# Value products in two passes of two query blocks, with a new order of copy, low part, exponent and scaling

## The reference

```python
q = einsum("btd,de->bte", rmsnorm(x), w_q)            # 16 heads of 64
s = einsum("bqhd,bkhd->bhqk", q_blk, k) * 64 ** -0.5  # blocks of 128 queries
s = s + fq_blk[..., :, None] - fk_t[:, :, None, :]    # forget bias
pr = softmax(where(kpos <= pos_blk, s, -inf))
o = einsum("bhqk,bkhd->bqhd", pr, v)
x = x + einsum("bte,ed->btd", o, w_o)
```

## Time and profile before

| | |
|---|---|
| median of 3 runs | 2847.16 us (2846.88 to 2847.24) |
| profiled execution | 2846.86 us, span 2845.0 us |
| PE busy | 2764.6 us (97%) |
| DVE busy | 1366.8 us (48%) |
| ACT busy | 836.1 us (29%) |
| attention pairs | from 1226 us to 1886 us of the span |

### The profile page before, as it was taken

One profiled execution on the slowest core, in us unless ns is written; L12 is line 12 of the kernel. 1 busy time (PEld: TensorE's weight loads), 2 busy tenths in 40 slices (PEclk: granted clock), 3 DMA queues, 4 the chain that ended last, 5 costly groups with the idle time before them and its releaser, 6 DMA issues.

```text
span 2845.0 us, 43288 instructions
## 1 busy us (share of the span) xinstructions
PE 2764.6 (97%) x18039; PEld 2693.4 (95%) x18039; DVE 1366.8 (48%) x1841; ACT 836.1 (29%) x1334; POOL 119.1 (4%) x82
## 2 busy tenths in 40 slices
PE   8999999999999999999999999879999999999998
PEld 8999999999999999989888889779999999999998
DVE  6876444344244244455556655554542442442444
ACT  6765221121111112334444444442211110111121
POOL 1000100000000000310000000002000000000000
PEclk9999999999999999999999999899999999999999
DMA  3113111111111111233322323111111111111112
GB/s 134 40 44 99 48 45 42 50 50 37 57 45 40 51 45 40 57 103 83 90 75 63 94 87 98 53 41 50 42 42 54 45 39 54 45 39 53 45 44 78
DMA packets 91342, 166.49 MB, mean 59 GB/s; under 512 B 18066, under 2 KB 55154, under 8 KB 91026
## 3 DMA queue, kind: packets, MB, share of 16 engines
q1 hardware_dynamic: 91154, 163.72, 19.1%
HBM read 141.60 MB, written 13.70 MB: 55 GB/s over the span
## 4 chain that ended last, share of the span: by engine, by line
PE 88%; DVE 4%; issue 4%; ACT 2%; DMA 1%; DVEq 0%; SPq 0%; ACTq 0%
PE psum L339 78%; PE psum L1160 2%; PE psum L1108 2%; PE psum L1132 2%; DVE SB L1565 1%; DMA NF<-nf_scratch 1%; PE psum L1090 1%; DVE PTL L1592 1%; PE psum L1147 1%; ACT PTH L888 0%; DVE X L1648 0%; ACT SB L872 0%; PE psum L958 0%; PE psum L1074 0%; PE psum L960 0%
## 5 line engine op out<-in xcount | busy, mean ns | idle before, releaser
L339 PE MATMUL psum<-XH,WH 128*128 128x352 f32 x2904 | 641.1, 329 | 1.8 <-issue 1.8
L339 PE MATMUL psum<-XH,WL 128*128 128x352 f32 x2904 | 628.2, 324 | 0.0
L339 PE MATMUL psum<-XL,WH 128*128 128x352 f32 x2904 | 627.6, 324 | 0.0
L321 ACT ACTIVATE WH<-WR 128x1024 fp32r<-128x1024 f32 (+2 forms) x217 | 215.4, 993 | 1037.0 <-PE psum L339 1025.1
L339 PEld LDWEIGHTS psum<-XH,WL 128*128 128x128 f32 x2904 | 498.3, 188 | 1.6
L339 PEld LDWEIGHTS psum<-XL,WH 128*128 128x128 f32 x2904 | 493.8, 188 | 1.6
L339 PEld LDWEIGHTS psum<-XH,WH 128*128 128x128 f32 x2904 | 488.7, 189 | 5.0 <-issue 2.3
L1448 DVE TENSOR_TENSOR X<-psum,X 128x1056 f32<-128x1056 f32 x63 | 79.2, 1257 | 371.2 <-PE psum L339 371.2
L330 DVE TENSOR_TENSOR WL<-WR,WH 128x1024 fp32r<-128x1024 f32 (+2 forms) x217 | 246.0, 1134 | 11.7 <-ACT WH L321 11.3
L339 PE MATMUL psum<-FYH,WH 128*128 128x352 f32 x1134 | 245.3, 324 | 0.0
L339 PE MATMUL psum<-FYH,WL 128*128 128x352 f32 x1134 | 244.5, 323 | 0.0
(11 more groups left out here) (228 smaller groups left out, 3266.3 us busy)
## 6 DMA issues: line engine op xcount, KB each, us to landing
WR<-in_wfi SPq DMA_DIRECT2D x96, 512.0 KB, 3.5
WR<-in_wfo SPq DMA_DIRECT2D x64, 384.0 KB, 3.0
WR<-in_wa SPq DMA_DIRECT2D x24, 512.0 KB, 3.6
WR<-in_wqkv SPq DMA_DIRECT2D x24, 512.0 KB, 4.8
X<-in_xT SPq DMA_DIRECT2D x16, 528.0 KB, 5.3
CC<-in_ck SPq DMA_DIRECT2D x128, 64.0 KB, 1.9
NF<-nf_scratch SPq DMA_DIRECT2D x16, 512.0 KB, 4.6
CC<-in_cv SPq DMA_DIRECT2D x128, 64.0 KB, 1.9
```

The costliest lines, as they stand in the source:

```text
L321: nc.scalar.activation(WH[:, par, 0:n], WR[:, par, 0:n], ACT.Copy).then_inc(w_hi, 1)
L339: mm = nc.tensor.matmul(psum[0:m, 3 * slot + c, 0:CH], w, x[:, k, c * CH:(c + 1) * CH], start=(k == 0 and part == 0), stop=(k == nk - 1 an ...
```

## The change

The value products are made for two query blocks at a time (a double, units 2d+1 and 2d+2, in the new order 7 6, 1 0, 5 4, 3 2). The values lie as low and high part side by side, 128 stationary columns, and each key block gets two matmuls of 256 moving columns: one with `PTH` and one with `PTL`. The results high and low stand in different halves of the PSUM partitions; ACT moves one half out (`o_half`), DVE adds the other (`add_halves`, `o_read`). The product of a double stands ahead of `turn` in its even slot, the decode product ahead of `turn(1)` in slot 2. In the pairs 0 to 6 ACT copies the high part of unit v-1 ahead of the exponent of v, and DVE takes its low part ahead of the scaling of v, from slot 2 on. The K tile is read in slot 12 behind the scaling. `KSTEPS` is spread anew. The PSUM homes are exchanged: `S_ps` 0 and 1, `O_ps` 2, projections 3 to 5, `T_ps` 6 and 7.

The last pair has code of its own: two `T_ps` (`T_alt` in the banks of the projections), its own second bias tile, logits one slot ahead, scaling and low part one slot later, the old order on ACT, and the splits of the first output tiles and the first output projection step inside it.

```diff
-BLOCKS = [7, 0, 6, 1, 5, 2, 4, 3]
+BLOCKS = [7, 6, 1, 0, 5, 4, 3, 2]
-KSTEPS = [2, 1, 2] + [1] * 14 + [3, 2]
+KSTEPS = [2, 1, 1, 1, 2, 1] + [1] * 6 + [2, 1, 1, 1, 1, 2, 2]
+PVS = 1 + NQB
@@ SyncE, pair
-                sp.wait_ge(s_read, u0 + 1 + NQB)
-                sp.dma_start(NF[:, :], ins["nf"][2 * hp + 1, :].partition_broadcast(P)).then_inc(nf_ld, 16)
+                if last:
+                    sp.wait_ge(k_out, 16 * NHP)
+                else:
+                    sp.wait_ge(s_read, u0 + 1 + NQB)
+                sp.dma_start((NF_last if last else NF)[:, :],
+                             ins["nf"][2 * hp + 1, :].partition_broadcast(P)).then_inc(nf_ld, 16)
@@ ScalarE, pair
+                    if v < 2 or c == NHP - 1:
+                        if v < UNITS:
+                            exponent(v)
+                        if v == 0:
+                            values_hi(c, t)
+                        copy_probs(v)
+                    else:
+                        copy_probs(v)
+                        if v < UNITS:
+                            exponent(v)
...
+                    elif v >= 5 and v % 2:
+                        d = (v - 5) // 2
+                        h = UNIT_OF[2 * d + 2][0]
+                        act.wait_ge(pv_done, PVS * c + d + 2 + 2 * PVS * t)
+                        nc.scalar.activation(out_double(d, hp), o_double(d)[HALF[1 - h], :],
+                                             ACT.Copy).then_inc(o_half, 1)
@@ ScalarE, last pair
+                    if c == NHP - 1 and v == UNITS - 1:
+                        act.wait_ge(qk_done, UNITS * NHP)
+                        act.wait_ge(k_out, 16 * NHP)
+                        o_split_hi(0)
+                    if c == NHP - 1 and v == UNITS:
+                        o_split_hi(1)
@@ TensorE, pair
+                def product(d):
+                    v = 2 * d + 2
                     h, i = UNIT_OF[v]
                     pe.wait_ge(pt_lo, (UNITS - 1) * c + v + 2 * (UNITS - 1) * t)
-                    pe.wait_ge(o_read, u0 + v)
-                    cols = slice(HD * h, HD * (h + 1))
-                    for kb in range(i + 1):
-                        keys = slice(P * kb, P * (kb + 1))
-                        for x, y, part in ((VH, PTH, 0), (VH, PTL, 1), (VL, PTH, 2)):
-                            mm = nc.tensor.matmul(O_ps[0:HD, 0:P], x[:, kb, cols], y[v % 2][:, keys],
-                                                  start=(kb == 0 and part == 0), stop=(kb == i and part == 2))
+                    if d == 0:
+                        pe.wait_ge(o_half, PVS * c + 1 + 2 * PVS * t)
+                    wait(pe, o_read, NQB * c + d + 2 * NQB * t if c or d else 0)
+                    for kb in range(i + 2):
+                        b = 0 if kb <= i else 1
+                        vv = VV[:, kb, 2 * h:2 * h + 2, :].rearrange("p a d -> p (a d)")
+                        for y, part in ((pt_buf(PTH, c, d), 0), (pt_buf(PTL, c, d), 1)):
+                            mm = nc.tensor.matmul(o_double(d)[:, P * b:2 * P], vv,
+                                                  y[:, kb, b:2, :].rearrange("p a q -> p (a q)"),
+                                                  start=(kb == 0 and part == 0), stop=(kb == i + 1 and part == 1),
+                                                  skip_group_check=True)
                     mm.then_inc(pv_done, 1)
+                if last:
+                    logits(0)
+                    values()
+                    logits(1)
+                    for v in range(1, UNITS + 2):
+                        if v + 1 < UNITS:
+                            logits(v + 1)
+                        if v == 2:
+                            decode_product()
+                        if v <= UNITS:
+                            turn(v - 1)
+                        if v == UNITS + 1:
+                            pe.wait_ge(w_ready, J_O + 1)
+                            pe.wait_ge(acc_read, J_O)
+                            pe.wait_ge(pt_lo, (UNITS - 1) * NHP - 1)
+                            o_k_step(0)
+                        if v >= 4 and v % 2 == 0:
+                            product((v - 4) // 2)
+                    return
                 for v in range(UNITS + 2):
                     if v < UNITS:
                         logits(v)
...
                     for _ in range(KSTEPS[v]):
                         project()
+                    if v == 2:
+                        decode_product()
+                    elif v >= 4 and v % 2 == 0:
+                        product((v - 4) // 2)
                     if 1 <= v <= UNITS:
                         turn(v - 1)
-                    if v >= 2:
-                        product(v - 2)
@@ VectorE, pairs 0 to 6
+                for v in range(UNITS + 1):
+                    if v < UNITS:
+                        maximum(v)
+                    if v - 1 in SPLIT_SLOTS:
+                        lo_weights(dve, J_QKV + 3 * c + 4 + SPLIT_SLOTS.index(v - 1), 6, t)
+                    if v == 5:
+                        dve.wait_ge(job_done, J_QKV + 3 * c + 4 + 6 * t)
+                        scaled(dve, 1, QS[:, :]).then_inc(acc_read, 1)
+                    if v >= 2:
+                        probs_lo(v - 1)
+                    if v < UNITS:
+                        normalise(v)
+                    if v == 12:
+                        dve.wait_ge(job_done, J_QKV + 3 * c + 5 + 6 * t)
+                        dve.wait_ge(k_out, 16 * (c + 1) + 32 * t)
+                        scaled(dve, 1, KS[:, :]).then_inc(acc_read, 1)
+                    if v == 0:
+                        values_lo(c, t)
+                    if v >= 5 and v % 2:
+                        add_halves(c, t, (v - 5) // 2)
+                    spread(v)
```

More of the change, by code:

```diff
@@ L859, in pair, with exponent, copy_probs @@
                     keys_hi(0, 0, 0)
-                for v in range(UNITS + 2):
+                def exponent(v):
+                    rows, n = (2 * NS, DK) if v == 0 else (P, P * (UNIT_OF[v][1] + 1))
+                    act.wait_ge(s_read, u0 + v + 1)
+                    nc.scalar.activation(SB[0:rows, v % 2, 0:n], SB[0:rows, v % 2, 0:n], ACT.Exp,
+                                         bias=nmax[0:rows, v:v + 1], scale=-1.0,
+                                         accum_out=lsum[0:rows, v:v + 1]).then_inc(e_done, 1)
+                def copy_probs(v):
+                    if v == 1:
+                        act.wait_ge(t_done, u0 + v)
+                        T0 = t_unit(c, 0)
+                        nc.scalar.activation(PTD[:, 0:4 * NS], T0[:, 0:4 * NS], ACT.Copy)
+                        nc.scalar.activation(PTD[0:NS, 4 * NS:6 * NS], T0[0:NS, 4 * NS:6 * NS],
+                                             ACT.Copy).then_inc(pt_hi, 1)
+                    elif 2 <= v <= UNITS:
+                        act.wait_ge(t_done, u0 + v)
+                        if v >= 4 and v % 2 == 0:
+                            act.wait_ge(pv_done, PVS * c + v // 2 - (c == NHP - 1) + 2 * PVS * t)
+                        nc.scalar.activation(pt_unit(PTH, c, v - 1), t_blocks(c, v - 1), ACT.Copy).then_inc(pt_hi, 1)
+                for v in range(UNITS + 3):
                     if v == 2:
@@ L868, in pair @@
                         keys_hi(c + 1, t, 0)
-                    if v < UNITS:
-                        rows, n = (2 * NS, DK) if v == 0 else (P, P * (UNIT_OF[v][1] + 1))
-                        act.wait_ge(s_read, u0 + v + 1)
-                        nc.scalar.activation(SB[0:rows, v % 2, 0:n], SB[0:rows, v % 2, 0:n], ACT.Exp,
-                                             bias=nmax[0:rows, v:v + 1], scale=-1.0,
-                                             accum_out=lsum[0:rows, v:v + 1]).then_inc(e_done, 1)
@@ new lines, in pair, with o_split_hi @@
+                    if c == NHP - 1 and v == UNITS:
+                        o_split_hi(1)
+            def o_split_hi(d):
+                nc.scalar.activation(YO[:, d, 0, :], X[:, d, :], ACT.Copy).then_inc(o_hi, 1)
+            over_pairs(act, pair)
+            o_split_hi(2)
+            act.wait_ge(pv_done, PVS * NHP)
+            act.wait_ge(v_out, 16 * NHP)
+            for d in range(3, KT - 1):
+                o_split_hi(d)
+            act.wait_ge(o_half, PVS * NHP)
+            act.wait_ge(o_read, NQB * NHP)
@@ new lines, in pair, with maximum @@
+                    add_halves(c - 1, t, NQB - 1)
+                def maximum(v):
+                    rows, n = (2 * NS, DK) if v == 0 else (P, P * (UNIT_OF[v][1] + 1))
+                    bias = DM if v == 0 else NF_last if c == NHP - 1 and v > NQB else NF
+                    wait(dve, t_done, u0 + max(v - 1, 0))
+                    if v in (1, 1 + NQB):
+                        dve.wait_ge(nf_ld, 16 * (2 * c + 1 + (v > 1)) + 64 * t)
+                    wait_apart(dve, qk_done, u0 + v + 1, logits_seen)
+                    nc.vector.tensor_tensor_reduce(
```

(9 more changed lines are left out.)

240 lines of the change are left out of this document (121 added, 119 removed).

## The result

The changed kernel takes **2861.5 us** (median of 5, 2857.2 to 2864.1) against 2847.2 before: +14.3 us, ratio 1.0043, interval 1.0028 to 1.0058. Run once more beside the experiments it took 2864.4 us, ratio 1.0064, interval 1.0047 to 1.0081. It is slower, as forecast, but by just under half of the 28.8 us forecast. The profiled execution took 2861.53 us with a span of 2859.7.

A forecast was written before the change was run, and what follows sets the result against it. The prediction took middle pairs as bound by PE (97% busy overall) and the last pair by the engine-to-engine chain. Span 2845.0 + 44 (seven pairs) - 15 (last pair) = 2874, forecast 2876 us, range 2851 to 2895.

The forecast's parts named there:

- Products: Value products on PE in a middle pair: 14.3 us before, 10.4 after, so 3.9 us less PE work.
- Waits: PE's waits in a middle pair: 14.2 us after the change against 3.7 before, 10.5 us more.
- turn 2: Transposes between blocks 7 and 6, first head: PE waits 1.7 us for the scaling behind copy and low part.
- logits 10: Second head's logits: the bias is loaded after the maximum of unit 8, so PE waits 1.8 us.
- additions, 8/10/14/16: Products in slots 8, 10, 14, 16 wait for the previous double's addition on DVE: 0.8, 0.4, 0.6, 1.3 us.
- K tile: V projection's first step, slot 13: PE waits 2.1 us because the K tile is read behind a late scaling.
- the layouts' difference: Middle pair laid out by hand at full clock, old against new order: +6.3 us a pair, +44 us over seven.
- The last pair: Last pair up to the first output projection step: 15 us gained, with 8 and 24 as ends.
- The chain is covered: Rival: in middle pairs only PE work counts, saving 3.9 us each, giving 2805 us; chance 0.09.
- Only the old length of chain counts: Rival: scaling as if ready before the low part, 2.7 us more per middle pair, giving 2851 us; chance 0.13.
- The waits bring the low clock: Rival: a further low-clock stretch after the decode product costs up to 3 us a pair, giving 2897 us; chance 0.12.
- Passes paced by weight loads: Rival: two-pass product matmuls take 0.19 us each, +4.8 us per pair on the forecast, giving 2910 us; chance 0.04.

The follow-up runs named there:

- e4: Changed kernel with output halves, their additions and the K tile's scaling moved ahead within their slots in pairs 0 to 6: 2833.0 us, ratio 0.9957.
- e5: e4 (new order kept) with the projection's steps spread anew over the slots: 2813.5 us, ratio 0.9879.
- e7: Kernel before with only the new order on ScalarE and VectorE, from slot 2 on in pairs 0 to 6: 2843.1 us, ratio 0.9990.
- e6: e4 with the old order and the projection's steps spread anew for that order: 2812.5 us, ratio 0.9880.
- e15: e6 with the projection's steps spread as in the changed kernel: 2819.2 us, ratio 0.9904.
- e1: Changed kernel with the old order on both ScalarE and VectorE in pairs 0 to 6: 2830.3 us, ratio 0.9949.
- e10: Changed kernel without the products with the probabilities' low parts in pairs 0 to 6, so its output differs: 2844.6 us, ratio 0.9984.
- e9: Changed kernel with only the output halves and their additions moved ahead within their slots in pairs 0 to 6: 2858.3 us, ratio 1.0038.
- e13: Changed kernel with only the K tile's scaling moved ahead of the low part in slot 12, pairs 0 to 6: 2849.1 us, ratio 1.0015.
- e2: Changed kernel with the old order on ScalarE alone in pairs 0 to 6: 2874.8 us, ratio 1.0100.
- e3: Changed kernel with the old order on VectorE alone in pairs 0 to 6: 2920.6 us, ratio 1.0264.
- e8: Changed kernel with its last pair run like the others: old order, one home for turned units, late output splits: 2891.1 us, ratio 1.0156.

## Why the prediction had the direction right and the size wrong

**Products: more saved than forecast.** I took 0.125 us for 256 columns; they take 0.120. I took 0.112 us for the 16 of 128 columns, from a decode product whose matmuls have 8 columns; they take 0.061 and 0.113 by turns. For this and the following terms I took, for each matmul of a pair, the middle value over seven pairs of the time to the next matmul's start. The products sum up to 15.0 us before (forecast 14.3) and 9.5 after (10.4): 5.5 us less and not 3.9. About 0.4 of the 15.0 is low clock: the first product of 24 matmuls, right behind the decode product, takes 1.9 us and, outside low clock, 1.4. The Trainium skill's rule (TensorE: Matmul & The Clock Gate, Back-to-back issue gap), by which it would have been 9.9, does not fit: the 98 ns estimated from that page stand against 120 measured.

**Waits: right in place, too large in size.** In the same sheet PE's waits over 0.2 us are, us a pair:

```
                      forecast  measured
turn 2                   1.7       0.6
turn 10                  1.7       1.7
turns 6, 14              1.6       1.7
logits 4                 0.9       0.8
logits 10                1.8       1.3
additions, 8/10/14/16    3.1       2.3   (0.9, 0, 0.4, 1.0)
K tile                   2.1       2.0
all waits, before        3.7       2.1
all waits, after        14.2      11.6
```

Each wait that was named is there, and turn 10, turns 6 and 14, logits 4 and the K tile came out within 0.1 us. The error is in turn 2, in logits 10 and in the additions, of which slot 10's doesn't show. The growth is 9.5 us a pair, not 10.5.

**Transposes and logits**, entered at no change, grew by 1.5 us a pair in amounts under 0.2 us each. Most of it is not gaps but clock: 0.9 us of it lies in slot 2, where the transposes of unit 1 now follow the decode product and run at low clock in four of the seven pairs. Typical pair: -5.5 + 9.5 + 1.5, about +5.4 (81.9 to 87.3).

**Low clock costs in full where PE sets the pace, and nothing where PE waits for the chain.** The layout has the full clock and left everything else as it was. To see what the clock does, take one slot in pairs that differ in it; columns as in the earlier trace rows. Slot 2 (logits 2, one step, decode product, turn 1) of pairs 2 and 3 in the changed kernel, where PE doesn't wait:

```profile
1410.64:1420.05 9.41, 9.41 (x58) 8.87 (x57) 3.06 (x5) 3.21 (x6) 1.90 (x1) 0.77 0.36 105
1503.75:1511.11 7.36, 7.36 (x58) 6.83 (x57) 3.06 (x5) 3.21 (x6) 0.14 (x1) 1.00 0.46 130
```

Slot 3 (logits 3, one step, turn 2) of pairs 0 and 4 there, then of pair 1 in e4, which has the same work in that slot:

```profile
1243.64:1248.94 5.30, 3.71 (x22) 3.11 (x20) 3.63 (x6) 3.84 (x5) 0.97 (x1) 0.86 0.44 123
1598.97:1604.28 5.31, 5.04 (x22) 4.29 (x20) 3.63 (x6) 3.42 (x5) 0.00 (x0) 0.57 0.44 126
1328.42:1333.62 5.20, 3.00 (x22) 2.47 (x20) 3.63 (x6) 3.85 (x5) 0.92 (x1) 1.00 0.40 114
```

PE is busy for 3.0 to 5.0 us in it, by the clock, and the slot takes 5.2 to 5.3 us all the same: the scaling sets its end. In e4's pair 1, at the full clock, turn 2 starts 1.7 us late, as laid out; in the changed kernel 1.1 of the 1.7 us are filled by PE's own slower work. In e5, where three steps stand in slot 3 and PE doesn't wait, it is 6.5 us at 0.83 and 7.5 at 0.71:

```profile
1570.19:1576.66 6.47, 6.47 (x40) 6.35 (x38) 3.64 (x6) 3.22 (x4) 1.35 (x1) 0.83 0.45 129
1649.87:1657.36 7.49, 7.49 (x40) 7.37 (x38) 3.63 (x6) 3.21 (x4) 1.90 (x1) 0.71 0.40 112
```

**The step that failed: the layouts' difference, +6.3 us a pair, entered as the growth of a pair.** The prediction read what the trace had above the layout (2.3 us in its pair, 2.4 on average) as the low clock behind the decode product, and left it as it was. But pair 4 of the kernel before had no low clock at all and took 82.3 us, not 81.0, longer than pair 5, which had it:

```profile
1563.78:1646.10 82.32, 79.19 (x636) 72.00 (x635) 48.36 (x100) 35.93 (x79) 5.69 (x3) 1.00 0.29 85
1646.10:1728.03 81.93, 80.01 (x636) 73.50 (x634) 48.12 (x100) 35.87 (x79) 5.69 (x3) 0.98 0.29 85
```

"Undisturbed" in the next table is a pair put together slot by slot, each slot at the middle length that it has in pairs where no low clock falls into it (where there is none such, in all pairs; slots 3 and 4 of before and slot 3 of the changed kernel hardly depend on it). us a pair:

```
                          laid out  undisturbed  measured  beyond the layout
before                      81.0      82.0         83.4     +2.4
e7, before + new order      81.4      81.4         82.8     +1.4
e5                          78.1      80.2*        81.1     +3.0
e6                          78.3      78.8*        80.6     +2.3
e15                         81.5      80.2         81.7     +0.2
e4                          83.2      82.1         83.2      0.0
e1                          83.8      82.0         83.2     -0.6
e10                         83.4      82.1         84.0     +0.6
e9                          85.0      84.1         86.2     +1.2
e13                         85.4      84.2         86.0     +0.6
changed, and again          87.2   85.9, 86.1   88.1, 88.4  +0.9, +1.2
e2                          90.0      86.9         89.4     -0.6
e3                          94.4      92.4         94.7     +0.3
* slot 3 has low clock in all pairs and pays for it
```

The forecast was 11 us too high in the seven pairs. Undisturbed, a pair grew by 4.0 us (81.96 to 85.94) where 6.3 were laid out: 2.3 too many, 16 us over seven pairs. The layout of before was 1.0 too short and that of the change 1.3 too long. In the prediction's terms the two that were mis-sized are the products (5.5 us saved, not 3.9, which is 11 us over seven pairs) and the waits (9.5 us more, not 10.5, which is 7, turn 2 above all, where low clock filled the wait). Against that, what low clock and scatter add to a pair was put at no change and grew from 1.4 to about 2.1 us, which gives 5 us back; PEclk pair by pair comes to about 5 us of low clock a pair before and 8 after. Of the other 3 us that the forecast was too high, 2 are the scatter ahead of the first pair, 1 the last pair and what is behind it. Why the layout of before is 1.0 us short although its waits (3.7 for 2.1) are too long stays open.

Some of the agreement between layouts and measured pairs is luck. In every kernel with many waits, and in e15, the layout is 1 to 3 us longer than the undisturbed pair, and low clock and scatter put 1.2 to 2.5 us on top of it. The two nearly cancel, and so e4 came out at its layout to the us. Where projection steps fill the waits, as in e5 and e6, nothing hides the low clock, and the pair comes out 2 to 3 us over the layout. The order of the kernels is right nearly everywhere all the same.

**The last pair: right.** Forecast -15, measured -15.7. The projection's first step starts 64.1 us after the pair's start (1840.71 to 1904.76), where 64.5 stood in the sum, with a wait of 1.2 us for the split tiles (1 forecast). The bound of 8 us was too careful, for e8 shows that the pair would have lost 11 us without its own order, its second home and its early splits, a loss that the forecast had not named.

**The rivals.** "The chain is covered" fell by the waits. "Only the old length of chain counts" gave 2851 us: the time is nearer to it (10 us) than to the forecast (15 us), but its mechanism is out, since the waits are for scalings, and undoing the order gave 31 us. "The waits bring the low clock" is half seen: there is more low clock, but part of it falls where PE waits anyway, and a pair lost 0.7 us more to clock and scatter, not 3. Passes paced by weight loads, at 0.19 us, fell by the 0.120 us.

## What to carry to other kernels

Lay a pair out on each engine by hand and name each wait with its cause: the places came true and led straight to a kernel 1.2% faster than before. Before trusting the sizes, check the layout against slots that ran at the full clock, and don't put a difference of two layouts on top of a trace unseen. Low clock under a wait is free, and it costs in full again once that wait is filled. A saving on the busiest engine can be lost when it takes away the cover of a chain between the others. After making one engine's work shorter, move the short steps that others wait for (an addition, a tile that frees PSUM) to the head of their slots, and spread the filling work anew. In this kernel, undoing an order of a chain on one of its two engines alone was worse than either order.

## What the runs showed of the hardware

- Matmuls on 128 wide weights with 256 columns (float32r, two operands in turn) take 0.120 us each from start to start at the full clock, a double of 16 takes 1.85 us; those of 128 columns on 64 wide weights take 0.060. Twice the weights and twice the columns, for twice the time.
- A slot in which PE waits for a scaling took 5.2 to 5.3 us at a granted clock of 0.57, 0.86 and 1.00 alike; one in which PE never waits took 7.4 us at 1.00 and 9.4 at 0.77.
- The last pair, with the first projection row, ran at a granted clock of 0.91 before, 0.93 after, and 0.82 in e8, where PE had most waits.
- Executions of one kernel differ with the granted clock: e10 took 2835.2 us at a mean clock of 0.988 and 2847.0 at 0.980. Single traces of two kernels are therefore comparable only stretch by stretch.
